# Feed-forwards three and four: one 512-column product for both parts of the activations against the high weights, the two halves of PSUM added afterwards

## The reference

```python
def _swiglu(x, w_in, w_out):
    gate, up = jnp.split(x @ w_in, 2, axis=-1)
    return (jax.nn.silu(gate) * up) @ w_out

h = h + 0.5 * _swiglu(_rmsnorm(h, ffn1_norm[i]), ffn1_w_in[i], ffn1_w_out[i])
...
h = h + 0.5 * _swiglu(_rmsnorm(h, ffn2_norm[i]), ffn2_w_in[i], ffn2_w_out[i])
```

## Time and profile before

| | |
|---|---|
| median of 3 runs | 1225.86 us (1224.7 to 1229.43) |
| the profiled execution's own time | 1226.63 us |
| its span | 1224.8 us |
| PE busy | 1192.5 us, 97%, 8139 products |
| PEld busy | 1105.2 us, 90% |
| DVE busy | 894.2 us, 73% |
| ACT busy | 682.8 us, 56% |
| DMA | 211.48 MB, 46.3% of 16 engines on the main queue |
| mean granted TensorE clock | 0.99 of 2.4 GHz |

### The profile page before, as it was taken

The page is one execution under the profiler, slowest core; times in us unless marked ns, Lnnn a source line. Parts: engine busy times, 40 slices in busy tenths (PEclk is TensorE's granted clock), DMA queues, the critical chain, the costliest instruction groups (busy, mean ns, idle before and its releaser), DMA issues.

```text
span 1224.8 us, 21613 instructions
## 1 busy us (share of the span) xinstructions
PE 1192.5 (97%) x8139; PEld 1105.2 (90%) x8140; DVE 894.2 (73%) x1712; ACT 682.8 (56%) x1206; POOL 3.5 (0%) x9
## 2 busy tenths in 40 slices
PE   9999999999999789999999999999999999999997
PEld 7989979999999667999999999999899889999985
DVE  6987878978778765897877765565789667556566
ACT  6954556655556763665554644443557655444454
POOL 0000000000000000000000000000000000000000
PEclk9999999999999999999999999999999999999998
DMA  9543333554555313365454455545354046554540
GB/s 349 204 177 140 119 138 139 222 193 169 202 181 212 123 53 155 142 220 194 168 203 180 180 214 197 183 176 204 140 184 166 30 165 236 191 191 169 205 155 35
DMA packets 21303, 211.48 MB, mean 173 GB/s; under 512 B 2624, under 2 KB 2880, under 8 KB 4480
## 3 DMA queue, kind: packets, MB, share of 16 engines
q1 hardware_dynamic: 20880, 208.90, 46.3%
q0 software_dynamic: 368, 1.84, 0.4%
HBM read 209.68 MB, written 1.05 MB: 172 GB/s over the span
## 4 chain that ended last, share of the span: by engine, by line
PE 92%; DVE 4%; ACT 3%; issue 1%; POOL 0%; ACTq 0%; POOLq 0%
PE ps L352 28%; PE ps L353 27%; PE ps L354 27%; PE ps L357 8%; ACT arena L983 1%; PE ps L449 1%; DVE h_lo L1584 1%; DVE x L1573 1%; DVE w_lo L1502 1%; ACT w_hi L983 0%; PE ps L593 0%; PE ps L783 0%; DVE arena L1861 0%; DVE arena L1810 0%; DVE arena L1812 0%
## 5 line engine op out<-in xcount | busy, mean ns | idle before, releaser
L1502 DVE TENSOR_TENSOR w_lo<-raw,w_hi 128x1024 fp32r<-128x1024 f32 (+1 forms) x390 | 448.5, 1168 | 71.5 <-ACT w_hi L983 71.2
L352 PE MATMUL ps<-h_hi,w_hi 128*128 128x256 f32 x1608 | 455.8, 283 | 0.0
L353 PE MATMUL ps<-h_lo,w_hi 128*128 128x256 f32 x1608 | 455.0, 283 | 0.0
L354 PE MATMUL ps<-h_hi,w_lo 128*128 128x256 f32 x1608 | 455.0, 283 | 0.0
L983 ACT ACTIVATE w_hi<-raw 128x1024 fp32r<-128x1024 f32 (+1 forms) x390 | 382.9, 1009 | 52.2 <-PE ps L354 48.3
L353 PEld LDWEIGHTS ps<-h_lo,w_hi 128*128 128x128 f32 x1608 | 308.3, 192 | 3.2
L352 PEld LDWEIGHTS ps<-h_hi,w_hi 128*128 128x128 f32 x1608 | 308.3, 192 | 3.2
L354 PEld LDWEIGHTS ps<-h_hi,w_lo 128*128 128x128 f32 x1608 | 308.3, 192 | 0.0
L352 PE MATMUL ps<-w_hi,y_hi 128*128 128x512 f32 (+2 forms) x550 | 211.4, 384 | 1.1 <-DVE y_lo L1872 1.0
L353 PE MATMUL ps<-w_lo,y_hi 128*128 128x512 f32 (+2 forms) x550 | 209.0, 380 | 0.0
L354 PE MATMUL ps<-w_hi,y_lo 128*128 128x512 f32 (+2 forms) x550 | 208.1, 378 | 0.0
(11 more groups left out here) (272 smaller groups left out, 980.2 us busy)
## 6 DMA issues: line engine op xcount, KB each, us to landing
raw<-in_stream SPq DMA_DIRECT2D x129, 1536.0 KB, 6.5
raw<-in_stream SPq DMA_DIRECT2D x3, 512.0 KB, 6.8
x<-in_x SPq DMA_DIRECT2D x2, 512.0 KB, 4.8
arena<-in_mem SPq DMA_DIRECT2D x1, 1024.0 KB, 13.4
x<-in_x POOLq DMA_DIRECT2D x1, 1024.0 KB, 5.3
out<-arena SPq DMA_DIRECT2D x4, 256.0 KB, 2.1
vec<-in_vectors SPq DMA_DIRECT2D x1, 633.0 KB, 8.1
arena<-in_final POOLq DMA_DIRECT2D x1, 512.0 KB, 3.8
```

The lines of the kernel that those rows point to most:

```text
L352: pe.matmul(o, lh, rh, start=start, stop=False, skip_group_check=True)
L353: pe.matmul(o, lh, rl, start=False, stop=False, skip_group_check=True)
L354: return pe.matmul(o, ll, rh, start=False, stop=stop, skip_group_check=True)
L1502: dve.tensor_tensor(w_lo[:, s, a], raw[:, s, a], w_hi[:, s, a], ALU.subtract).then_inc(s_lo, 1)
```

## The change

In feed-forwards 2 and 3 (`BOTH`), for chunks 1 to 21, `up` becomes `up_both`. `h_hi` and `h_lo` now lie side by side in `h_both` [128, 8, 2, 256], so that one product of 512 columns takes both against `w_hi`: high x high lands in columns 0 to 255 of a bank, low x high in columns 256 to 511. A second product of 256 columns adds high x `w_lo` to the first half. A half z now needs a bank of its own, taken in turn from banks 4, 5 and 6 (`half_bank`), so PE has to wait until the half three before it has been read: a new wait for `tu_done` ahead of each half. ACT copies columns 256 to 511 of both halves to SBUF (`second`), DVE adds them to columns 0 to 255 from PSUM, and then multiplies by `rb` in place. ACT's `hi` of piece 1 moves ahead of Silu. Chunk 0 and feed-forwards 0 and 1 keep their products.

```diff
-        h_hi = sb("h_hi", [P, KT, S], F32R)
-        h_lo = sb("h_lo", [P, KT, S], F32R)
+        h_both = sb("h_both", [P, KT, 2, S], F32R)
+        h_hi, h_lo = h_both[:, :, 0, :], h_both[:, :, 1, :]
...
+        BOTH = (2, 3)
+        def half_bank(j, z):
+            return 4 + (2 * j + z + 2) % 3
...
+                def up_both(j, z):
+                    s, b = (U0 + j) % SLOTS, half_bank(j, z)
+                    for k in range(KT):
+                        a = slice(z * PIECE + k * P, z * PIECE + k * P + P)
+                        full(ps[:, b, :], w_hi[:, s, a], h_both[:, k, :, :].rearrange("p a b -> p (a b)"), k == 0, k == KT - 1)
+                        m = full(ps[:, b, 0:S], w_lo[:, s, a], h_hi[:, k, :], False, k == KT - 1)
+                    return m
...
                     for z in range(2):
                         pe.wait_ge(s_lo, lo_at(r, j, z))
-                        for k in range(KT):
-                            m = up_part(j, z, k)
+                        if i in BOTH:
+                            n = max(2 * j + z - 3, 1) + 1 + 2 * n0
+                            pe.wait_ge(sem("tu_done"), n if r is None else r * 6 + n)
+                            m = up_both(j, z)
+                        else:
+                            for k in range(KT):
+                                m = up_part(j, z, k)
...
     (ACT, plain feed-forward)
+                        both = i in BOTH and (r is not None or j > 0)
+                        if both:
+                            act.wait_ge(sem("up_ready"), at(r, n0 + j + 1))
+                            for z in range(2):
+                                m = copy(second(i)[:, g, z * S:(z + 1) * S], ps[:, half_bank(j, z), S:2 * S])
+                            m.then_inc(sem("part_done"), 1)
+                            if r is not None or j < CH - 1:
+                                hi(r, U0 + j + 2, 1)
                         act.wait_ge(sem("tu_done"), at(r, 2 * (n0 + j) + 1, 6))
                         act.activation(sa[:, g, :], tu[:, g, 0:S], ACT.Silu).then_inc(sem("silu_done"), 1)
-                        if r is not None or j < CH - 1:
+                        if not both and (r is not None or j < CH - 1):
                             hi(r, U0 + j + 2, 1)
...
     (DVE)
+                    if i in BOTH and (r is not None or j > 0):
+                        sums = []
+                        dve.wait_ge(sem("part_done"), part_at(r, i, j))
+                        for z in range(2):
+                            sums.append(chain.inc(dve.tensor_tensor(tu[:, g, z * S:(z + 1) * S],
+                                                                    ps[:, half_bank(j, z), 0:S],
+                                                                    second(i)[:, g, z * S:(z + 1) * S], ALU.add)))
+                        for z in range(2):
+                            dve.wait_ge(s_chain, chain.at(sums[z]))
+                            v = tu[:, g, z * S:(z + 1) * S]
+                            dve.tensor_tensor(v, v, rb, ALU.mult).then_inc(sem("tu_done"), 1)
+                    else:
...
```

More of the change, by code:

```diff
@@ L239, in build, with second @@
         g_abs = A(8056, T, 256)
+        def second(i):
+            return cv if FFNS[i][1] is None else A(7680, 3, 512)
         cv, sa, gg, tu = A(0, 3, 512), A(1536, 3, S), A(2304, 3, S), A(6144, 3, 512)
@@ L250, in build, with part_at @@
         FFN_NORM = (1, 3, 4, 6)
+        BOTH = (2, 3)
+        def half_bank(j, z):
+            return 4 + (2 * j + z + 2) % 3
+        def part_at(r, i, j):
+            n = BOTH.index(i) * (CH - 1) + j
+            return n if r is None else r * 3 + n
         LATE, EARLY = (1, 2, 3, 4, 6, 7), (0, 5, 8)
@@ L1602, in body @@
                     dve.wait_ge(sem("up_ready"), at(r, n0 + j + 1))
-                    for z in range(2):
-                        dve.tensor_tensor(tu[:, g, z * S:(z + 1) * S], ps[:, b, z * S:(z + 1) * S], rb,
-                                          ALU.mult).then_inc(sem("tu_done"), 1)
+                    if i in BOTH and (r is not None or j > 0):
+                        sums = []
[4 more added lines that the diff above has]
+                                                                    second(i)[:, g, z * S:(z + 1) * S], ALU.add)))
+                        for z in range(2):
+                            dve.wait_ge(s_chain, chain.at(sums[z]))
+                            v = tu[:, g, z * S:(z + 1) * S]
+                            dve.tensor_tensor(v, v, rb, ALU.mult).then_inc(sem("tu_done"), 1)
+                    else:
+                        for z in range(2):
+                            dve.tensor_tensor(tu[:, g, z * S:(z + 1) * S], ps[:, b, z * S:(z + 1) * S], rb,
+                                              ALU.mult).then_inc(sem("tu_done"), 1)
                     if cw:
@@ L1659, in ffn @@
                 with dve.Fori(0, (CH - 1) // 3 - 1) as r:
-                    chain.enter(r, 9 if cw else 0)
+                    chain.enter(r, (9 if cw else 0) + (6 if i in BOTH else 0))
                     for j in range(1, 4):
```

## The result

| | before | with the change |
|---|---|---|
| median | 1228.70 us (22 runs, 1224.70 to 1234.72) | 1235.30 us (22 runs, 1227.53 to 1237.94) |
| span of the profiled execution | 1224.8 us | 1236.1 us |
| PE busy | 1192.5 us, 8139 products | 1198.6 us, 7468 products |
| DVE busy | 894.2 us | 919.6 us |
| ACT busy | 682.8 us | 710.3 us |

The ratio of the two kernels is 1.0045, 95% interval 1.0031 to 1.0059: the change makes the kernel 5.5 us slower (3.8 to 7.2; the means of the 22 runs each are 5.6 us apart, the medians 6.6). That is under the 0.5% which the prediction took as the least that can be told from no change, but clear of zero.

The account below looks back on a forecast made before the run. PE bounds the kernel, by the distances between its products' starts. Products -8.1, wait +6.4, clock +2.0 and 0 elsewhere sum to +0.3 us: forecast 1226.2 us, no measurable change, range 1217.5 to 1232.5 (own range 1223 to 1234).

Parts of the forecast that it names:

- The wait at the second chunk: Ahead of chunk 1 in feed-forwards 2 and 3, PE waits 3.2 us each for chunk 0's multiplications: together 6.4 us.
- The products: In both feed-forwards, 672 groups of three products become two, 348 instead of 360 ns each: 8.1 us saved.
- The clock: Behind each wait at chunk 1 the granted clock falls to 0.50: 1.0 us each, 2.0 us together, bounds 0 and 3.4.
- ACT, DVE, the end of a feed-forward: Added copies and additions never make PE wait in the steady loop; the last chunk's low part just fits: 0 us.
- a wait at every chunk: Rival: DVE's additions come late, so half 1 of the next chunk finds its bank full: 1238.8 us; chance 0.06.
- a product at the fillers' distance: Rival: merged product comes at the fillers' 217 ns, saving 15.1 us, while the wait costs 6.4: 1218.2 us; chance 0.06.
- a wait that isn't paid: Rival: at chunk 1 PE does not wait and the clock stays up: 1217.8 us; chance 0.09.
- The third: Rival: a product is charged by its columns, so merging saves only 1.7 to 3.4 us: 1231.8 us; chance 0.08.

Follow-up runs that it names:

- wait_only: The kernel before plus only PE's wait for both `tu_done` of chunk 0 ahead of chunk 1 in feed-forwards 2 and 3: 1238.33 us, ratio to before 1.0085.
- dve_first: The changed kernel, waits kept, with DVE multiplying chunk 0 ahead of its third piece of weights in feed-forwards 2 and 3: 1229.13 us, ratio to before 1.0003.
- no_first_wait: The changed kernel without the wait ahead of chunk 1, all waits from chunk 2 on kept: 1226.87 us, ratio to before 0.9978.
- no_wait_early_hi: As `no_first_wait`, with ACT's high piece 1 of chunk 0 also made ahead of Silu: 1224.92 us, ratio to before 0.9970.
- grouped: `no_wait_early_hi` with products in pairs of feature blocks, two of 512 columns, then two of 256: 1221.01 us, ratio to before 0.9942.
- warm_in_wait: The changed kernel with 13 filler products between `spread` and chunk 1 in feed-forwards 2 and 3: 1230.82 us, ratio to before 1.0016.
- all_four: `no_wait_early_hi` with the merged product in all four feed-forwards: 1230.79 us, ratio to before 1.0018.

## Why the prediction was wrong

The range held the result, 1231.4 us on the scale of the forecast (1225.86 x 1.0045), but "no change, 1226.2" was not what came: the kernel is slower by an amount clear of noise. The sum had four terms; two were right and two mis-sized in the same direction. The step that failed is the price of the merged product: the prediction took the distance behind a 512-column product as its own, whatever stands next to it, and the runs show that it depends on the neighbours.

- **The wait at the second chunk, 6.4 us: right.** 3.2 us in both feed-forwards, read from code and from DVE's row in the trace of before. `wait_only` shows it alone, `dve_first` shows that DVE's list sets its length, `no_first_wait` that the change didn't need it.
- **The products, -8.1 us: too much; it is 4.7** (`no_wait_early_hi`). The term took 228 ns, the average over the twelve down products, and 120 ns for the other, so 12 ns saved. In alternation the pair costs 352.5 ns, not 348. A hint stood in the trace of before: of the twelve down products the first five, right behind 256-column ones, are 232 ns apart and the last seven 226. The prediction used such a number only as a bound. The row of the sixth, between those of the earlier trace rows:

```profile
762.56 0.39 PE L354 MATMUL ps<-w_hi,y_lo 128*128 128x512 f32 x1
```

The 348 ns do exist, in `grouped`. The rule of the Trainium skill (TensorE: Matmul & The Clock Gate, "Wait — 56ns, not 53.3ns?"), by which merging saves 2.5 ns, would have given 1.7 us; the trace stands between it and my 12 ns, at 7.

- **The clock, 2.0 us: too little; it is about 3.** One fall was measured at 1.4 to 1.5 us in `wait_only`, where I had put 1.0 a piece, so 2.9 for two. In the profiles it came behind six of the eight waits of 1.8 to 3.0 us at the start of a feed-forward. The runs give 3.5 (`warm_in_wait` against the changed kernel), with the wide interval said there; the bound of 3.4 for both is not contradicted.
- **ACT, DVE, the end of a feed-forward, 0: right.** No `tu_done` makes PE wait past chunk 1. From DVE's timeline in the steady loop, as in the earlier trace rows:

```profile
723.76 0.76 DVE L1649 TENSOR_TENSOR arena<-ps,arena 128x256 f32<-128x256 f32 x2 [2.54 <-ACT arena L1012]
724.43 0.75 DVE L1655 TENSOR_TENSOR arena<-arena 128x256 f32<-128x256 f32 x2
```

DVE still idles 2.54 us ahead of a chunk's sums. The margin at the end, forecast as "just fits", held in the plain feed-forwards, and is what gives way in `all_four`.

With the sizes of the other runs' stretches: -4.7 + 6.4 + 2.9 = +4.6 us, against 5.5 measured (3.8 to 7.2). The products were 3.4 us off, the clock 0.9, and both point to slower; the 0.9 us left over is inside the interval. Of the rivals, a wait at every chunk did not come, nor did a product at the fillers' distance, nor a wait that isn't paid. The third, "the fixed price doesn't go", forecast 1231.8, next to the 1231.4 measured, but that is in part luck: more of the price went than it said (4.7 us, not 1.7 to 3.4), and the clock cost more.

## What to carry to other kernels

A wait of the engine that bounds a kernel costs its length and, on TensorE, often the clock behind it: here 3.2 us became nearly 5 in `wait_only`. When a change rotates buffers, check the first turns one by one, for there a clamped index asks for more than the buffer needs, and the engine that must answer may have a list of its own ahead of the answer. And once a product is merged, try the order in which the widths follow each other: the same products in pairs of a kind gave 8.75 us where alternation gave 4.7.

## What the runs showed of the hardware

- The distance between products depends on the neighbours. 512 and 256 columns in turn: 352.5 ns for the two. In twos of a kind: 348 ns. In a row of eight: 1.81 / 8 = 226 ns and 0.96 / 8 = 120 ns in the first half of a chunk, where the wide ones follow other wide ones, and 1.84 / 8 = 230 ns in the second half, where they follow narrow ones. Why alternation costs 4.5 ns was not settled.
- The clock fell behind a wait as short as 1.8 us (`dve_first`, feed-forward 2), and did not behind the same wait in feed-forward 3, nor behind 3.0 us in feed-forward 3 of the changed kernel. One profile doesn't tell what a wait costs in clock.
- The runs of one kernel spread over up to 10 us (1224.70 to 1234.72 for the kernel before). Most of the spread of the changed kernel's runs goes with the mean granted clock, and the profiles put most of their differences ahead of feed-forward 1, where the clock is low in the latent attention.
